# The order of row tiles in a single-core sparse-attention stage: ascending, or interleaved in pairs of a small and a large tile

## The reference

```python
score = where(causal, score, -inf)          # indexer score of each key
_, sel = top_k(score, 256)                  # 256 keys for each query row
logits = einsum('bqhd,bqkd->bhqk', qb, k_sel) * Dh ** -0.5
logits = logits - slopes[h] * (q_pos - sel)
p = softmax(where(sel <= q_pos, logits, -inf))
out = einsum('bhqk,bqkd->bqhd', p, v_sel)   # 8 heads share k and v
```

## Time and profile before

| | |
|---|---|
| median of 3 runs | 1658.06 us (1655.67 to 1660.11) |
| the profiled execution, its time | 1658.34 us |
| its span, first to last instruction | 1656.5 us |
| mean granted TensorE clock | 0.952 |
| PE / DVE / ACT / POOL busy, share of span | 90% / 60% / 44% / 24% |
| load of one q tile (512 KB), issue to landing | 4.8 us median |
| attention stage, first logits matmul to first `ga0` matmul | 612.23 to 786.55 us, 174.3 us |

### The profile page before, as it was taken

One profiled execution on the slowest core, in us unless ns is written; L12 is line 12 of the kernel. 1 busy time (PEld: TensorE's weight loads), 2 busy tenths in 40 slices (PEclk: granted clock), 3 DMA queues, 4 the chain that ended last, 5 costly groups with the idle time before them and its releaser, 6 DMA issues.

```text
span 1656.5 us, 19621 instructions
## 1 busy us (share of the span) xinstructions
PE 1496.2 (90%) x7262; PEld 1230.9 (74%) x7262; DVE 1000.2 (60%) x1466; ACT 730.7 (44%) x1175; POOL 397.4 (24%) x367
## 2 busy tenths in 40 slices
PE   6989999997999878999999999999984789999980
PEld 5877888886888765676888878888861677778860
DVE  3339999999996856764000013356135777889964
ACT  5247123526233436765112233333132677788850
POOL 2310222363213261000222223222220212121104
PEclk9999999998999988999999999999997899999995
DMA  5200111131311121110211133443333768786668
GB/s 185 59 25 1 45 46 41 31 108 33 83 40 38 51 89 51 52 39 13 83 51 51 58 114 136 151 146 110 127 144 123 281 257 309 254 346 211 221 241 304
DMA packets 83500, 196.68 MB, mean 119 GB/s; under 512 B 10574, under 2 KB 32334, under 8 KB 81102
## 3 DMA queue, kind: packets, MB, share of 16 engines
q1 hardware_dynamic: 68430, 146.67, 27.0%
q0 software_dynamic: 11232, 40.90, 6.7%
q10 hardware_dynamic: 3744, 7.87, 1.3%
HBM read 198.55 MB, written 40.89 MB: 145 GB/s over the span
## 4 chain that ended last, share of the span: by engine, by line
PE 77%; DVE 9%; DMA 6%; ACT 4%; issue 3%; SPq 1%; POOL 1%; ACTq 0%; POOLq 0%; DVEq 0%
PE ps L643 21%; PE ps L645 21%; PE ps L644 21%; PE ps L842 3%; DMA e_raw<-in_w_up 3%; DVE dist L1359 2%; PE ps L832 2%; DVE e_lo L1626 1%; DMA t_y<-y_dram,slot 1%; PE ps L898 1%; PE ps L771 1%; PE ps L859 1%; ACT junk L1073 1%; DMA xin<-in_x 1%; PE ps L784 1%
## 5 line engine op out<-in xcount | busy, mean ns | idle before, releaser
L1691 POOL TENSOR_TENSOR w_lo<-w_raw,w_hi 128x512 fp32r<-128x512 f32 (+1 forms) x160 | 216.9, 1358 | 696.5 <-ACT w_hi L963 696.0
L963 ACT CAST w_hi<-w_raw 128x512 fp32r<-128x512 f32 (+1 forms) x160 | 97.5, 615 | 501.4 <-PE ps L645 465.4
L643 PE MATMUL ps<-w_hi,n_hi 128*128 128x512 f32 (+2 forms) x704 | 245.0, 348 | 8.7 <-POOL w_lo L1691 6.8
L645 PE MATMUL ps<-w_hi,n_lo 128*128 128x512 f32 (+2 forms) x704 | 243.4, 346 | 0.0
L644 PE MATMUL ps<-w_lo,n_hi 128*128 128x512 f32 (+2 forms) x704 | 243.2, 345 | 0.0
L1626 DVE TENSOR_TENSOR e_lo<-e_raw,e_hi 128x2048 fp32r<-128x2048 f32 x93 | 210.1, 2285 | 17.4 <-ACT e_hi L1253 16.4
L1472 DVE TENSOR_TENSOR a_lo<-a_raw,a_hi 128x1024 fp32r<-128x1024 f32 x32 | 40.1, 1255 | 291.1 <-ACT a_hi L1204 290.9
L1253 ACT CAST e_hi<-e_raw 128x2048 fp32r<-128x2048 f32 x93 | 176.2, 1915 | 49.8 <-DMA e_raw<-in_w_up 49.7
L1396 DVE MAX8 small<-dist 128x8 f32<-128x384 f32 (+5 forms) x192 | 171.8, 895 | 6.6
L643 PE MATMUL ps<-n_hi,w_hi 128*128 128x512 f32 x448 | 175.6, 392 | 0.0
L644 PE MATMUL ps<-n_lo,w_hi 128*128 128x512 f32 x448 | 174.7, 390 | 0.0
(11 more groups left out here) (244 smaller groups left out, 2694.0 us busy)
## 6 DMA issues: line engine op xcount, KB each, us to landing
e_raw<-in_w_gate SPq DMA_DIRECT2D x62, 512.0 KB
e_raw<-in_w_up SPq DMA_DIRECT2D x62, 512.0 KB
e_raw<-in_w_down SPq DMA_DIRECT2D x31, 1024.0 KB
w_raw<-in_w_in SPq DMA_DIRECT2D x72, 256.0 KB, 2.7
y_dram<-e_y POOLq DMA_DIRECT2D x31, 512.0 KB, 4.0
a_raw<-att_dram SPq DMA_DIRECT2D x16, 512.0 KB, 3.5
a_raw<-ret_dram SPq DMA_DIRECT2D x16, 512.0 KB, 3.5
w_raw<-in_w_in SPq DMA_DIRECT2D x40, 128.0 KB, 2.4
```

What stands on the lines that cost most here:

```text
L643: mm(out, a[0], b[0], start=first, stop=False, skip_group_check=skip)
L645: return mm(out, a[1], b[0], start=False, stop=last, skip_group_check=skip)
L963: nc.scalar.copy(w_hi[c % NH][:, :width], w_raw[c % NR][:, :width]).then_inc(hi_ready, 1)
L1691: G.tensor_tensor(w_lo[c % NH][:, :width], w_raw[c % NR][:, :width], w_hi[c % NH][:, :width].bitcast(F32), ALU.subtract).then_inc(lo_ready, 1)
```

## The change

The tiles are taken in the order 0, 7, 1, 6, 2, 5, 3, 4 (`ORDER`), in pairs j = 2p, 2p+1. Inside a pair four heads of the small tile are followed by four heads of the large one, then the other four of the small, then of the large. `head_at(m)` gives (place j in `ORDER`, head h) of step m. The lags between the parts of a head (2 steps to the transposes, 6 to P·V) stay, as do all instructions, their number and their shapes. What else moves:

- q halves are turned in step m with m % 4 == 1, one in each group of four heads. In the groups of the small tile it is the first or second half of the odd place of the pair (r = 0) or the first half of the next pair's small tile (r = 2); in the groups of the large tile the second half of the pair's large tile (r = 1) or of the next small tile (r = 3).
- Loads and stores of q and of the output take rows `ORDER[j]`; SP issues the load of place 2 ahead of its loop, and of place j+3 in pass j, ahead of its waits for P·V of place j.
- `q1` is computed in the order of `ORDER`, so that tiles 0 and 7 are the two that stay in `qrow`; norm factors are made for tiles 0, 7 and then 1 to 6.
- `prob` and `small` columns are chosen by m instead of h, `pT` by j % 2 instead of by the half of heads.

```diff
+ORDER = [0, 7, 1, 6, 2, 5, 3, 4]
...
+        def head_at(m):
+            p, r = divmod(m // 4, 4)
+            return 2 * p + r % 2, r // 2 * 4 + m % 4
+
         def q_turned_at(m):
-            return (m // HA + 1, m % HA // 2 - 1) if m % HA in (3, 5) and m // HA + 1 < NT else None
+            p, r = divmod(m // 4, 4)
+            j = 2 * p + (2 if r >= 2 else 1)
+            return (j, r % 2) if m % 4 == 1 and j < NT else None
...
-            for t in range(NT):
-                if t + 2 < NT:
-                    load_q(t + 2)
+            load_q(2)
+            for j in range(NT):
+                if j + 3 < NT:
+                    load_q(j + 3)
                 for g in range(2):
-                    bk.wait_read(sp, ("pv", t, g))
+                    bk.wait_read(sp, ("pv", j, g))
...
                         if kind in ("R", "M"):
-                            t = slice(b * P, (b + 1) * P)
+                            row = ORDER[b] if name == "q1" else b
+                            t = slice(row * P, (row + 1) * P)
...
             for m in range(STEPS + 6):
                 if m < STEPS:
-                    t, h = divmod(m, HA)
-                    nk = (t + 1) * P
+                    j, h = head_at(m)
+                    nk = (ORDER[j] + 1) * P
                     name = ("lg", m)
                     bk.wait_free(pe, name)
-                    if h == 0:
-                        for g in range(2):
-                            bk.wait_read(pe, ("qT", t, g))
+                    if h % 4 == 0:
+                        bk.wait_read(pe, ("qT", j, h // 4))
...
                 if 2 <= m < STEPS + 2:
-                    t, h = divmod(m - 2, HA)
+                    t = ORDER[head_at(m - 2)[0]]
                     pe.wait_ge(p_done, m - 1)
...
                 if pv_at(m):
-                    t, g, part = pv_at(m)
-                    name = ("pv", t, g)
+                    j, g, part = pv_at(m)
+                    t = ORDER[j]
+                    name = ("pv", j, g)
                     if part == 0:
                         bk.wait_free(pe, name)
                         for i in range(t // 4 + 1):
-                            bk.wait_read(pe, ("pT", HA * t + 4 * g + 3, i))
+                            bk.wait_read(pe, ("pT", m - 3, i))
...
-                    scale_q(t, 1)
+                    scale_q(ORDER[t], 1)
                     scale_rows(t)
                 pool.wait_ge(q_squares, NT)
-                scale_q(2, NT - 2)
+                scale_q(1, NT - 2)
```

More of the change, by code:

```diff
@@ L486, in program @@
             if 2 <= m < STEPS + 2:
-                for i in range((m - 2) // HA // 4 + 1):
+                for i in range(ORDER[head_at(m - 2)[0]] // 4 + 1):
                     bk.use(("pT", m - 2, i), 4 + i)
@@ L839, in _ @@
                         for i in range(t // 4 + 1):
-                            bk.wait_read(pe, ("pT", HA * t + 4 * g + 3, i))
+                            bk.wait_read(pe, ("pT", m - 3, i))
                     for kt in range(part * (t + 1) // 4, (part + 1) * (t + 1) // 4):
-                        last = mm(bank(name), kvu[:, kt, DH:2 * DH], pT[:, kt, g], start=kt == 0, stop=kt == t)
+                        last = mm(bank(name), kvu[:, kt, DH:2 * DH], pT[:, kt, j % 2], start=kt == 0, stop=kt == t)
                     if part == 3:
@@ L1057, in out_q @@
                     bk.wait_full(act, ("ro", HR - 1, 3))
+                rows = ORDER if b else range(NT)
                 places = [qrow[t][:, 4:8].rearrange("p h d -> p (h d)") if b == 1 and t < 2 else (qst1 if b else qst0)[t][:]
@@ L1065, in out_q @@
                     bk.wait_read(act, (f"q{b}", t))
-                    act.dma_start(q_dram[t * P:(t + 1) * P, b * BANK:(b + 1) * BANK], places[t]).then_inc(q1_stored if b else q0_stored, 16)
+                    act.dma_start(q_dram[rows[t] * P:(rows[t] + 1) * P, b * BANK:(b + 1) * BANK], places[t]).then_inc(q1_stored if b else q0_stored, 16)
             def square_q0():
@@ L1161, in _ @@
                 if m < STEPS:
-                    t, h = divmod(m, HA)
-                    nk = (t + 1) * P
+                    j, h = head_at(m)
+                    nk = (ORDER[j] + 1) * P
                     act.wait_ge(mx_done, m + 1)
-                    A(prob[h % 4][:, :nk], prob[h % 4][:, :nk], ACT.Exp, bias=small[:, 128 + h:129 + h],
-                      scale=2.0 ** -(h + 1), accum_out=small[:, 144 + h:145 + h]).then_inc(ex_done, 1)
+                    A(prob[m % 4][:, :nk], prob[m % 4][:, :nk], ACT.Exp, bias=small[:, 128 + m % 8:129 + m % 8],
+                      scale=2.0 ** -(h + 1), accum_out=small[:, 144 + m % 8:145 + m % 8]).then_inc(ex_done, 1)
                 if pv_at(m) and pv_at(m)[2] == 3:
@@ L1184, in _ @@
                         n = min(4, t + 1 - 4 * i)
-                        bk.read(nc.scalar.copy(pT[:, 4 * i:4 * i + n, g, h % 4 * P:(h % 4 + 1) * P],
+                        bk.read(nc.scalar.copy(pT[:, 4 * i:4 * i + n, j % 2, h % 4 * P:(h % 4 + 1) * P],
                                                bank(name, n * P).rearrange("p (k q) -> p k q", q=P)), name)
@@ L1390, in out_q1 @@
                     seq(V.tensor_tensor(q_sq[t % 2][:], src, src, ALU.mult))
-                    V.tensor_reduce(small[:, S_QR + HA * t + 4:S_QR + HA * (t + 1)], q_sq[t % 2][:], X, ALU.add).then_inc(q_squares, 1)
+                    V.tensor_reduce(small[:, S_QR + HA * ORDER[t] + 4:S_QR + HA * (ORDER[t] + 1)], q_sq[t % 2][:], X, ALU.add).then_inc(q_squares, 1)
             def take_rounds(sc, first, end):
@@ L1447, in _ @@
                     if m >= 4:
-                        for i in range((m - 4) // HA // 4 + 1):
+                        for i in range(ORDER[head_at(m - 4)[0]] // 4 + 1):
                             bk.wait_full(dve, ("pT", m - 4, i))
@@ L1719, in scale_rows @@
                 pool.wait_ge(q_in[t % 2], 16 * (t // 2 + 1))
-                G.tensor_tensor(qrow[t % 2][:], qrow[t % 2][:], small[:, S_QR + HA * t:S_QR + HA * (t + 1)].unsqueeze(2).to_broadcast([P, HA, DH]),
+                G.tensor_tensor(qrow[t % 2][:], qrow[t % 2][:], small[:, S_QR + HA * ORDER[t]:S_QR + HA * (ORDER[t] + 1)].unsqueeze(2).to_broadcast([P, HA, DH]),
                                 ALU.mult).then_inc(q_scaled, 1)
```

37 lines of the change are left out of this document (19 added, 18 removed).

## The result

The kernel after takes 1666.11 us in the median of 20 runs (1659.90 to 1670.40), the kernel before 1659.03 us in 20 runs beside it (1654.50 to 1668.75). The ratio is 1.0032 [1.0017, 1.0048]: **slower by 0.3%**, just beyond the bound at which I had called two times the same.

A forecast was written before the change was run, and what follows sets the result against it. Large tiles were taken as PE-bound, small heads as waiting on the PE-DVE-ACT round, 22.6 us lost. After: 15.5 + 5.5 + 1.0 + 2.0 (clock) = 24.0 lost, 1.4 more than before's 1658.34: 1660.0 us, range 1651 to 1667.

The forecast's parts named there:

- my own signs: Stage: still 172 to 178 us, PE gaps of 2.5 to 3 us at steps 8 and 16, one clock dip.
- waits change places: Stage: waits leaving small tiles return in large groups; 22 to 26 us lost, total 1657 to 1662; chance 0.49.
- 15.5 us: Large-to-small passages: PE's waits for DVE's scaling summed over the four pairs, 3.4 + 3.3 down to 0.6 + 0.
- chain's 6.5 us: Pair 0/7, from step 14's logits: DVE, ACT and cast until step 14's scaling reaches PE, against 3.5 us of PE work.
- Start: 5.5 us: Stage's start: 3.5 us lost in tile 0's first steps plus 2.0 at half clock; bounds 4.5 and 7.
- small to large at nothing: Small-to-large passages: the large tile's P·V covers the small heads' short chains, so no cost.
- I take one fall at 2.0 us: Clock: one fall to half speed in the long gaps, costing 2.0 us; lower bound 0, upper 2.7.
- slower rival: Behind large groups of pairs 0/7 and 1/6: two to four clock falls at 2.7 us; 1663 to 1668, middle 1666; chance 0.27.
- q loads, POOL, SP, q1 ... All of it 0: Loads, POOL's factor operation, SP's order and q1's addresses: no cost; a late load 2 to 5 us once.
- short DVE outliers: Within the slower rival: DVE delays that large tiles hid before, about 1 us each.
- Drain ... 1.0 us, as before: Stage's end, last group now tile 4: shorter chain but P·V waits for the same copies; 1.0 us lost.
- faster one: Large groups: each gap costs 1 us or less, 8 instead of 15.5, no clock fall; total 1649; chance 0.24.

The follow-up runs named there:

- e1: Kernel after with second q halves turned in the small group's last step instead of inside the large group; 1657.12 us, ratio to before 0.9989.
- e6: Kernel after with POOL's scaling of the q tiles of places 3, 5 and 7 held back by some steps; 1664.70 us, ratio to before 1.0037.
- e2: Kernel after with 8 additional PE matmuls, results unread, in the first steps behind large groups; 1665.09 us, ratio to before 1.0041.
- e9: Same kernel as e5, run again on another chip; 1652.64 us, ratio to before 0.9961.
- e5: Kernel after with second q halves turned in the small group, and lags of 3 steps to transposes, 7 to P·V; 1652.27 us, ratio to before 0.9966.
- e7: Kernel after with both second q halves turned in the small group and POOL's scaling held back; 1657.34 us, ratio to before 0.9986.
- e0: Kernel after run again with no edit; 1665.47 us, ratio to before 1.0039.
- e8: e5 with the order of the pairs reversed (3, 4, 2, 5, 1, 6, 0, 7) and POOL's factor operation split to suit; 1657.31 us, ratio to before 0.9978.
- e3: Kernel after with transposes 3 steps behind the logits instead of 2, and P·V 7 instead of 6; 1662.42 us, ratio to before 1.0006.

## Why the prediction was right and wrong

**The range held, and that is in part luck.** By my own signs the sum was wrong: the stage was to take 172 to 178 us and takes 182.4, with three dips of the clock in place of one; it was to grow by 1.4 us and grew by 8.1. The mechanism came as forecast, several of its terms were too small, and the range was wide enough by 0.9 us.

**Right: waits change places.** The stage loses what the small tiles gained, in front of the large tile's transposes, behind DVE's scaling, shrinking from pair to pair. The signs for it came: 2.76 and 2.42 us at steps 8 and 16 (2.5 to 3 forecast), 3.89 us between two maxima (about 4). e1 shows that the cause is the one I had named, the q half's cast and subtraction between two maxima: moving it alone takes 10.6 to 11.2 us off the stage, the falls that went with the gaps included.

**Near in its sum, too high in its parts: "15.5 us" behind large groups.** The listed idle there is 14.4 us in after, but POOL's part is in it. Without POOL in these places (e6) it is 11.9. The chain's 6.5 us were met at step 14; what was too small was PE's side of it, 4.1 us where I had counted 3.5. Yet the blocks without collision or fall (28 to 35, 44 to 59; in e6 those from step 20 and 36, 2.7 and 2.0 us lost) come out 0.1 to 0.3 us above the forecast. So something beside the listed waits is lost, perhaps in the pipeline's end and restart at each wait; no run shows what.

**Right: "Start: 5.5 us", small to large at nothing.** The first block lost 10.7 us where 10.9 were forecast; as its fall cost 1.3 us and not 2.0, the rest of it was 0.5 us too cheap. No wait of more than 0.3 us stands in front of a small tile's transposes. The clock rose at 621, and before at 630: with tile 7 as early as step 4, PE was at full speed 9 us sooner. That gain of the new order stays, and it was in the sum.

**Wrong: "I take one fall at 2.0 us."** After 622 the clock fell three times in one profile of after and twice in the other. Each costs 1.3 us (e2, two blocks), 1.34 (e9 against e5) or 1.5 (the fifth block of after against its repetition): together 3.9 to 4.1 us for three and 2.6 for two, against 2.0. The price of one was too high, the number too low. The slower rival had the mechanism ("two to four falls") at 2.7 each: right in number, twice too dear.

**Wrong: "q loads, POOL, SP, q1 ... All of it 0."** This is the step that failed. I looked at POOL for late q tiles, and none came late. What POOL does to DVE I had not priced, although the trace of before shows it: the 1.78 us scaling at 694.05. There PE's work covered all but 0.66 us of it, the only idle time of PE in tile 5; in the new order two scalings of rows fell on the passages, and cost 0.8 (1.7 in the second profile) and 1.6 us. The slower rival names "short DVE outliers" of 1 us, without their cause. The third fall at 723 stands at the gap that POOL widened from 1.13 (e6) to 2.63 us.

**Slightly small: "Drain ... 1.0 us, as before".** It is 1.4 by the same count, and the last block is the same in all runs of the paired order with this lag (18.98 to 19.00 us). Two waits are listed in it: 0.68 us for ACT's copy at 789.34, which before has too (0.68 at 779.99), and 0.44 for DVE's scaling at 785.63, which before has not.

The excess of 6.7 us is thus: falls 1.9 to 2.1, POOL 2.4, drain 0.4; 1.8 to 2.0 us stay unplaced, spread over the blocks with 0.1 to 0.5 us in each. With the 1.4 us of the forecast the excess makes 8.1, as in the stage (8.1), against 7.1 in the medians (1666.11 - 1659.03).

**The rivals.** The faster one needed gaps of 1 us or less and no fall. e1 and e5 come near it, at 1657 and 1652 us, with no fall but with gaps up to 1.78 and 1.41 us, and after an edit that the change does not contain. Its reason, that DVE and ACT have room, was true and did not help: the fixed order on their queues decided. The slower one was the case that came, at 1666.11 beside its middle of 1666, by less than it said from the clock and more from POOL; that the two meet so closely is chance.

**Open:** why a gap of 2.63 us at 723 was followed by a fall and one of 2.70 was not, and the same for e9 and e5. The gap's length alone does not decide it. Open too is what the ascending order would gain from moved turns.

## What to carry to other kernels

When the order of work changes, list per engine queue what stands between an operation and the one that the bottleneck waits for, at each passage from long steps to short ones: one conversion placed there cost more than the reordering could bring; moved to the short steps, with one step more of lag, it turned +0.3% into -0.35%. Price the other engines' effect on durations as well as their lateness, from outliers in the old trace that something happens to cover. And count a possible fall of the clock at each long gap, here at about 1.3 us each, rather than one for all.

## What the runs showed of the hardware

- DVE's scaling from SBUF to SBUF is held up by POOL's operation until that ends: 2.12 us in place of 0.62 for 768 columns, and 1.95 us in place of 0.29 for 128 columns, beside a POOL operation of 1.90 us. The delay follows POOL when that is moved (e6, e7).
- The clock dropped to 0.50 in, or within 0.8 us behind, gaps of 2.76, 2.42 and 2.63 us (after; the first two also in e0 and e6), 2.15 (e8), 1.48 with one of 1.66 ahead of it (e3), 1.41 (e3, at 656.59), and 0.97 with ones of 1.40 and 1.20 ahead of it (e9). It stayed at 1.00 after 2.70 (e0), 2.63 (e7), 1.83 (e0 and e2) and 1.78 us (e1). Identical code with nearly the same gaps did either.
- Such a fall inside dense work lasted 3.4 us in after, three times (631.2 to 634.6, 655.1 to 658.5, 723.4 to 726.8), and cost 1.3 to 1.5 us; PE regained full speed each time while it went on working.
